# Retention prompt: both halves of the output multiplied ahead of the final state instead of behind it

## The reference, cut to what matters

```python
def step(s, inp):
    qc, kc, vc = inp
    a = jnp.einsum('bnhk,bmhk->bhnm', qc, kc) * decay
    o = (jnp.einsum('bhnm,bmhv->bnhv', a, vc)
         + jnp.einsum('bnhk,bhkv->bnhv', qc, s) * xi[None, :, :, None])
    s = g_c[None, :, None, None] * s + jnp.einsum('bmhk,bmhv->bhkv', kc * zeta[None, :, :, None], vc)
    return s, o
```

## Time and profile before

| | |
|---|---|
| median of 3 runs | 1846.43 us (1844.65 to 1847.4) |
| profiled execution | 1845.82 us, of it 1843.7 us from the first to the last instruction (the span) |
| busy share of the span | PE 97%, PEld 92%, DVE 51%, ACT 47%, POOL 47% |
| mean granted TensorE clock | 0.988 of 2.4 GHz |
| line 1732 / 1736 / 1743, instructions | 64 / 64 / 128 |
| line 1135 (copy of the state) | 8 times, median 1.225 us |

### The profile page before, as it was taken

How to read it: one execution, slowest core, us unless ns; L and a number is a source line. 1 busy time by engine, 2 the same in 40 slices (tenths; PEclk the granted TensorE clock), 3 DMA queues, 4 the chain that set the end, 5 groups by cost and what they waited for, 6 DMA issues and landing times.

```text
span 1843.7 us, 33029 instructions
## 1 busy us (share of the span) xinstructions
PE 1781.0 (97%) x14520; PEld 1688.2 (92%) x14520; DVE 947.4 (51%) x1035; ACT 870.4 (47%) x1020; POOL 861.6 (47%) x246
## 2 busy tenths in 40 slices
PE   8999999999979999999999988999999999999998
PEld 7988888999969999998989878999998888889998
DVE  4344446675486753334444355776243444377743
ACT  4455455444454344455445445434454555543443
POOL 3555455544215554664444402355355554545551
PEclk9999999999989999999999979999999999999999
DMA  8777854555334555856555532454667778545552
GB/s 274 251 254 269 298 201 159 183 183 182 116 115 157 175 180 177 239 160 185 146 167 145 167 96 92 139 176 161 205 213 272 250 265 292 206 141 175 175 182 87
DMA packets 306036, 346.36 MB, mean 188 GB/s; under 512 B 7847, under 2 KB 269479, under 8 KB 305887
## 3 DMA queue, kind: packets, MB, share of 16 engines
q1 hardware_dynamic: 264528, 266.59, 45.5%
q10 hardware_dynamic: 41367, 77.67, 11.8%
HBM read 299.67 MB, written 44.82 MB: 187 GB/s over the span
## 4 chain that ended last, share of the span: by engine, by line
PE 88%; DVE 5%; ACT 2%; POOL 2%; DMA 1%; issue 1%; ACTq 0%; DVEq 0%
PE acc L1501 22%; PE acc L1508 21%; PE acc L1502 21%; PE mix L1643 2%; PE mix L1902 2%; POOL w_lo L1405 2%; PE mix L1732 1%; PE mix L1563 1%; PE mix L1875 1%; PE acc L1529 1%; PE acc L1530 1%; PE acc L1535 1%; PE mix L1632 1%; PE mix L1662 1%; DMA st<-in_state_ret_dram 1%
## 5 line engine op out<-in xcount | busy, mean ns | idle before, releaser
L1405 POOL TENSOR_TENSOR w_lo<-raw,w_hi 128x2048 fp32r<-128x2048 f32 (+2 forms) x181 | 777.3, 4299 | 592.0 <-ACT w_hi L466 592.0
L1501 PE MATMUL acc<-g_hi,w_hi 128*128 128x264 f32 x2544 | 639.3, 289 | 4.3 <-DVE gate L1190 2.9
L1502 PE MATMUL acc<-g_lo,w_hi 128*128 128x264 f32 x2544 | 628.1, 284 | 0.0
L466 ACT ACTIVATE w_hi<-raw 128x2048 fp32r<-128x2048 f32 (+3 forms) x260 | 456.0, 1755 | 177.1 <-PE acc L1508 77.9
L1501 PEld LDWEIGHTS acc<-g_hi,w_hi 128*128 128x128 f32 x2544 | 478.9, 188 | 15.8 <-issue 13.6
L1502 PEld LDWEIGHTS acc<-g_lo,w_hi 128*128 128x128 f32 x2544 | 481.4, 189 | 1.4
L950 DVE TENSOR_TENSOR w_lo<-raw,w_hi 128x2048 fp32r<-128x2048 f32 (+2 forms) x79 | 334.6, 4235 | 234.6 <-ACT w_hi L466 234.6
L1508 PE MATMUL acc<-g_hi,w_lo 128*128 128x264 f32 x2544 | 342.2, 285 | 0.0
L1508 PEld LDWEIGHTS acc<-g_hi,w_lo 128*128 128x128 f32 x2544 | 325.3, 188 | 2.4 <-issue 1.3
L1439 POOL TENSOR_TENSOR h_lo<-hid,h_hi 128x528 fp32r<-128x528 f32 x44 | 59.3, 1347 | 330.3 <-ACT h_hi L737 330.3
L1501 PE MATMUL acc<-h_hi,w_hi 128*128 128x264 f32 x664 | 164.0, 284 | 0.0
(11 more groups left out here) (248 smaller groups left out, 2256.6 us busy)
## 6 DMA issues: line engine op xcount, KB each, us to landing
raw<-in_w_ffn_in_dram SPq DMA_DIRECT2D x88, 1024.0 KB, 5.2
raw<-in_w_in_ret_dram SPq DMA_DIRECT2D x48, 1024.0 KB, 6.7
raw<-in_w_in_attn_dram SPq DMA_DIRECT2D x36, 1024.0 KB, 6.3
st<-in_state_ret_dram ACTq DMA_DIRECT2D x64, 512.0 KB, 6.4
out_dram<-st ACTq DMA_DIRECT2D x64, 512.0 KB, 6.6
raw<-in_w_ffn_out_dram SPq DMA_DIRECT2D x32, 768.0 KB, 4.2
raw<-in_w_ffn_out_dram SPq DMA_DIRECT2D x32, 640.0 KB, 4.8
raw<-in_w_out_ret_dram SPq DMA_DIRECT2D x16, 1024.0 KB, 7.9
```

The source lines that it names most:

```text
L466: A(w_hi[:, u % SPL, 0:size[u]], raw[:, u % RAW, 0:size[u]], ACT.Copy).then_inc(hi_split, 1)
L1405: TT(w_lo[:, u % SPL, 0:size[u]], raw[:, u % RAW, 0:size[u]], w_hi[:, u % SPL, 0:size[u]].bitcast(F32), ALU.subtract).then_inc(lo_by_pool, 1)
L1501: MM(out, wh, x_hi[:, ks[k], :], start=first and k == 0, stop=False)
L1502: MM(out, wh, x_lo[:, ks[k], :], start=False, stop=False)
```

## The change

The four lines that multiply the state, and the signal behind them, move from ahead of the two output groups to behind them. No instruction is added, removed or altered, and every wait stays with the instruction that it stood before; the state's products still follow the waits for `vrow_ready` and `v_stack_ready`.

```diff
                         if s == 5:
                             pe.wait_ge(vrow_ready, gh + 1)
                             pe.wait_ge(v_stack_ready, gh + 1)
-                            for kt in range(2):
-                                for c in range(2):
-                                    ins = MM(mix[:, 2 + kt, :], kz[:, c, kt * P:(kt + 1) * P], vrow[:, c, :],
-                                             start=(c == 0), stop=(c == 1))
-                            ins.then_inc(s1_done, 1)
                             for vt in range(4):
                                 ins = MM(mix[:, 1, vt * P:(vt + 1) * P], vrow[:, 0, vt * P:(vt + 1) * P],
                                          scoresT[:, 0, :], start=True, stop=True)
...
                                     ins = MM(mix[:, 0, vt * P:(vt + 1) * P], vrow[:, ck, vt * P:(vt + 1) * P],
                                              scoresT[:, j, :], start=(ck == 0), stop=(ck == 1))
                             ins.then_inc(o_done, 1)
+                            for kt in range(2):
+                                for c in range(2):
+                                    ins = MM(mix[:, 2 + kt, :], kz[:, c, kt * P:(kt + 1) * P], vrow[:, c, :],
+                                             start=(c == 0), stop=(c == 1))
+                            ins.then_inc(s1_done, 1)
```

## The result

The changed kernel takes 1851.62 us (median of 9 runs, 1848.46 to 1854.22) against 1846.79 us for the kernel before (9 runs, 1844.65 to 1850.18): 4.8 us more, a ratio of 1.0026 with a 95% interval of 1.0016 to 1.0037. The forecast was 1851.1.

The account below looks back on a forecast made before the run. Matrix work on TensorE fills 97% of the span, so only its waits count. Waits of 0.25, 0.25 and 1.86 us, 2.36 a layer, add 4.7 us in two layers to 1846.43: 1851.1, range 1848.0 to 1855.0.

Parts of the forecast that it names:

- The delay of the copy: VectorE's copy of the state out of PSUM (line 1135) starts 2.67 us later, behind 24 short matmuls.
- First spread, no wait: TensorE's first line 1632 broadcast after the state's copy keeps 0.4 us of cover at 8 places, so no wait.
- Second spread, heads 1 and 2: TensorE's second line 1632 broadcast behind these heads waits for the first sample update: 0.25 us each.
- Second spread, head 3: TensorE's second line 1632 broadcast behind this head waits for the first sample update: 1.86 us a layer.
- The vector engine's overlap of 0.09 us: Unwaiting vector instructions start 0.09 us before the previous one's recorded end, so room is 1.27 and 0.66 us.
- the other reading: Each vector instruction waits until the pipeline is empty, without overlap; the summed loss would be 0.5 us larger.
- Total: TensorE's losses of 2.36 us a layer, in two retention layers, add 4.7 us to the whole run.
- Cost nothing: ScalarE and GpSimd: ScalarE's output split and next weight split move about 1.2 us later; 7 us of cover, GpSimd's the same.
- Rival 1: Output projection behind head 3: lost time is given back at a late state load, between 1848.8 and 1847.0; chance 0.20.
- Rival 2: The 0.4 us cover before each head's first broadcast is too thin: +6.6 to 7.1 us, 1853.0 to 1853.5; chance 0.10.
- Rival 3: ScalarE's earlier output copies let its queue run ahead, removing TensorE's 4.1 us of update waits: 1842.3; chance 0.04.

Follow-up runs that it names:

- head 3 alone: State products moved behind the outputs in the fourth head of each layer only, the others as in the kernel before: 1849.37 us, ratio 1.0015.
- the norm first: Changed kernel with the previous head's last two group-norm steps (lines 1090, 1092) put ahead of the state's copy in VectorE's queue: 1846.35 us, ratio 0.9998.
- the attempt above: Kernel before with broadcasts alternating between two PSUM banks and ScalarE's weight split moved ahead of the last state's store: 1853.93 us, ratio 1.0037.
- the old order with the norm first: Kernel before with lines 1090 and 1092 put ahead of the state's copy in VectorE's queue: 1845.69 us, ratio 0.9997.
- the two banks: Kernel before with the broadcasts of line 1632 alternating between PSUM banks 2 and 3: 1847.18 us, ratio 1.0001.

## Why the prediction was right

- *The delay of the copy.* Worked out as 24 loads of 0.111 us, 2.67; measured 2.68 behind every head (5.34 - 2.66, behind head 0 of each layer 5.41 - 2.73).
- *First spread, no wait.* Right behind all eight heads; behind head 3 the distance from block to spread is unchanged at 8.05 us.
- *Second spread, heads 1 and 2.* Foretold 0.25 us, measured 0.27 and 0.26 (brackets of 0.20 and 0.21).
- *Second spread, head 3.* Foretold 1.86 us, measured 1.87 in both layers, and 1.87 with head 3 alone (brackets of 1.80).
- *The vector engine's overlap of 0.09 us.* The first update starts 0.08 us before the recorded end of line 1074 (232.61 against 232.01 + 0.68 = 232.69), without any idle time. By the other reading, with 0.5 us more, the second spreads would have come 5.2 us later in all; they came 4.8 later.
- *Total.* Foretold 4.7 us, measured 4.8, of which the two retention layers hold 4.6 in the one profiled execution. The interval of the ratio spans 3.0 to 6.8 us, so that the two times agree to 0.1 us is in part luck; the second spreads, term by term, are the finer check. The time that TensorE waits for updates was foretold as 8.8 us and is 8.6 by the brackets.
- *Cost nothing: ScalarE and GpSimd.* `ro_hi` stood at 120.96 and is at 121.86, the next weight split at 122.88 and is at 123.79. Head 1's block starts 0.36 us earlier in the second execution (111.70 against 112.06), so from the block both moved by about 1.26 us, the 1.2 us foretold, and nowhere near their cover.

Rival 1, the give-back at the late state load, was there in small: in the profiled execution the wait ahead of the last sample's spread is 0.82 us in layer 0, where it was 1.13, but 1.38 in layer 3, where it was 1.16. In the kernel with the norm first it is 2.11 in layer 0. This load's landing varies from one execution to the next by more than the change moves it, so neither a give-back nor a further loss can be read from it. Rival 2's margin of 0.4 us held: behind head 3 the copy ends at 229.63 and the first spread's load is at 230.02. Rival 3 fell: ScalarE does copy the outputs earlier, then waits for line 1092:

```profile
112.92 0.60 ACT L662 ACTIVATE y<-mix 128x512 f32<-128x512 f32 x1 [1.90 <-PE mix L1731]
...
121.86 1.09 ACT L597 ACTIVATE ro_hi<-y 128x1056 fp32r<-128x1056 f32 x1 [4.60 <-DVE y L1092]
```

## What to carry to other kernels

When two groups of products change places on an engine that is busy all the time, look first whether their own time changes (here it didn't); then ask which readers get their data later, and follow each reader's queue, in order, to the first thing that the busy engine needs back. There the room is the idle time ahead of that instruction plus the slack behind it, and the loss is the delay less the room; where the room is large (head 0) the same delay is free. Such a loss can be taken away in the reader's queue as well (put what doesn't depend on the late data ahead of it), but each such move starts other work at another time, and that can collide.

## What the runs showed of the hardware

*VectorE beside GpSimd.* Line 1090, a float32 multiplication with both inputs in SBUF, takes 1.25 us behind the copy, in the kernel before and in the changed one. With the norm first it took 4.03 us, from 112.73 to 116.76, beside GpSimd's subtraction:

```profile
111.12 4.53 POOL L1405 TENSOR_TENSOR w_lo<-raw,w_hi 128x2048 fp32r<-128x2048 f32 x1 [4.21 <-ACT w_hi L466]
```

GpSimd's ended at 115.65 and VectorE's 1.1 us behind it, nearly its usual length; in the attempt above GpSimd's ended at 260.23 and line 1093 at 261.32, again 1.1 us behind. So VectorE's instruction looks as if held until GpSimd's was over. The kernel before shows it more often, with line 950, VectorE's own weight subtraction of 2048 columns, also with both inputs in SBUF:

```profile
1128.26 4.58 POOL L1405 TENSOR_TENSOR w_lo<-raw,w_hi 128x2048 fp32r<-128x2048 f32 x1 [7.05 <-ACT w_hi L466]
1131.51 3.48 DVE L950 TENSOR_TENSOR w_lo<-raw,w_hi 128x2048 fp32r<-128x2048 f32 x1 [5.30 <-ACT w_hi L466]
...
22.55 2.29 DVE L950 TENSOR_TENSOR w_lo<-raw,w_hi 128x2048 fp32r<-128x2048 f32 x1
22.89 6.36 POOL L1405 TENSOR_TENSOR w_lo<-raw,w_hi 128x2048 fp32r<-128x2048 f32 x1 [21.39 <-ACT w_hi L466]
```

Of its 46 such instructions 8 have no subtraction of GpSimd beside them and take 2.29 us each. 37 start 0.4 to 3.3 us behind the start of GpSimd's; they take 3.48 to 6.32 us, and each ends 2.14 to 2.16 us behind GpSimd's end, whenever it began. One starts ahead of GpSimd's (22.55): it takes its 2.29 us, and GpSimd's takes 6.36 instead of 4.6. So whichever of the two subtractions starts second is held until the first is over. The page "SBUF — State Buffer" of the Trainium skill, section "SBUF: two separate sides", says that a vector instruction with two SBUF inputs and a GpSimd instruction take a shared port as an exclusive lock, the later one blocked until the first is through; these rows agree.

*The clock in the attention layer.* Of the twelve profiled executions nine spend 390.2 to 391.6 us there and three 393.2 to 394.9, the changed kernel's among them, and the order of the retention products has no part in it: the other two, the old order with the norm first and with the two banks, have the order of before. The granted clock goes with it: over 900 to 950 us it is 0.93 in the changed kernel and 1.00 in the kernel before. The changed kernel, in windows of 5 us:

```profile
935.00:940.00 5.00, 3.64 (x26) 3.19 (x25) 3.72 (x4) 1.10 (x2) 2.67 (x1) 0.98 0.98 311
940.00:945.00 5.00, 5.00 (x21) 4.14 (x21) 1.91 (x2) 1.81 (x3) 0.00 (x0) 0.50 0.95 215
```

The kernel before, at the same place:

```profile
932.00:937.00 5.00, 3.64 (x30) 3.28 (x29) 4.53 (x5) 0.66 (x2) 3.51 (x1) 1.00 0.82 252
937.00:942.00 5.00, 5.00 (x36) 4.53 (x37) 2.49 (x4) 2.02 (x4) 0.00 (x0) 1.00 1.10 270
```

Both wait once, for 1.36 us of the 5, at the same instruction; in one the clock then falls to half (1.2 GHz), in the other it stays at 2.4. That such a pause may or may not cost some 3 us may be part of the spread of the single runs, and is why a span of one execution (8.1 us here) is no measure of a change of 5.
